# DeltaNet building phase: gate projections beside the substitution, raw blocks in a tile of their own, the second group gathered ahead

## The reference, cut to what matters

```
m = where(strict, (k*beta) @ k.T * decay, 0)
sol = triangular_solve(m + I, [v*beta, k*beta*exp(cum)], lower, unit_diagonal)
attn = where(incl, q @ k.T * decay, 0)
# then step by step over the chunks, with the carried state s:
v_new = u - w @ s;  o = q_dec @ s + attn @ v_new;  s = s*chunk_decay + k_end.T @ v_new
```

## Time and profile before

| | us |
|---|---|
| runs before: median of 3 (lowest, highest) | 2170.61 (2168.0, 2174.12) |
| the profiled execution's own time | 2176.57 |
| its span | 2174.5 |
| mean granted TensorE clock | 0.896 |
| PE busy | 1782.7 (82%) |
| DVE busy | 1175.5 (54%) |
| ACT busy | 837.2 (39%) |
| POOL busy | 321.5 (15%) |

### The profile page before, as it was taken

The page is one execution under the profiler, slowest core; times in us unless marked ns, Lnnn a source line. Parts: engine busy times, 40 slices in busy tenths (PEclk is TensorE's granted clock), DMA queues, the critical chain, the costliest instruction groups (busy, mean ns, idle before and its releaser), DMA issues. The chain is left out here.

```text
span 2174.5 us, 20430 instructions
## 1 busy us (share of the span) xinstructions
PE 1782.7 (82%) x7774; PEld 1221.8 (56%) x7774; DVE 1175.5 (54%) x1356; ACT 837.2 (39%) x1101; POOL 321.5 (15%) x402
## 2 busy tenths in 40 slices
PE   6897889965896838497989889991399999999981
PEld 3344654465454727493434773550288888888861
DVE  3612922168224265364432341337798888888873
ACT  4112222321224426263200000342277777777762
POOL 0000300021000324710040430320011010101000
PEclk9998989978898959798969899995699999999996
DMA  8712000020000442231041213213399999999964
GB/s 348 249 69 79 1 1 0 0 79 1 0 0 0 148 138 85 71 86 67 0 140 39 78 71 134 72 54 126 131 384 395 387 385 402 381 402 386 400 240 174
DMA packets 102569, 337.20 MB, mean 155 GB/s; under 512 B 32170, under 2 KB 41949, under 8 KB 77769
## 3 DMA queue, kind: packets, MB, share of 16 engines
q1 hardware_dynamic: 96048, 317.16, 38.6%
q0 software_dynamic: 4608, 16.78, 3.1%
q10 hardware_dynamic: 1817, 1.97, 0.3%
HBM read 303.83 MB, written 32.04 MB: 154 GB/s over the span
## 5 line engine op out<-in xcount | busy, mean ns | idle before, releaser
L2702 DVE TENSOR_TENSOR w_lo<-w_raw,w_hi 128x2048 fp32r<-128x2048 f32 x192 | 438.5, 2292 | 65.3 <-ACT w_hi L2648 65.2
L2648 ACT ACTIVATE w_hi<-w_raw 128x2048 fp32r<-128x2048 f32 x192 | 367.8, 1917 | 137.4 <-PE ps L2606 134.1
L482 PE MATMUL ps<-hT,w_mixer 128*128 128x512 f32 (+1 forms) x864 | 344.9, 560 | 4.4 <-PEq L186 2.5
L482 PEld LDWEIGHTS ps<-hT,w_mixer 128*128 128x128 f32 x864 | 165.3, 193 | 173.9 <-issue 169.1
L2604 PE MATMUL ps<-w_hi,xsT_hi 128*128 128x512 f32 x512 | 202.8, 396 | 2.4 <-DVE xsT_lo L2707 2.4
L2606 PE MATMUL ps<-w_hi,xsT_lo 128*128 128x512 f32 x512 | 200.4, 391 | 0.0
L2605 PE MATMUL ps<-w_lo,xsT_hi 128*128 128x512 f32 x512 | 200.2, 391 | 0.0
L2431 PE MATMUL ps<-w_out,yT 128*128 128x512 f32 x256 | 114.3, 602 | 3.4 <-DMA router<-in_moe_router 3.4
L2604 PEld LDWEIGHTS ps<-w_hi,xsT_hi 128*128 128x128 f32 x512 | 96.8, 189 | 22.0 <-DVE xsT_lo L2707 2.8
L2606 PEld LDWEIGHTS ps<-w_hi,xsT_lo 128*128 128x128 f32 x512 | 96.5, 189 | 20.3
L2605 PEld LDWEIGHTS ps<-w_lo,xsT_hi 128*128 128x128 f32 x512 | 96.7, 189 | 19.3
(11 more groups left out here) (443 smaller groups left out, 2880.7 us busy)
## 6 DMA issues: line engine op xcount, KB each, us to landing
w_raw<-in_moe_w_gate SPq DMA_DIRECT2D x64, 1024.0 KB, 7.0
w_raw<-in_moe_w_up SPq DMA_DIRECT2D x64, 1024.0 KB, 8.8
w_raw<-in_moe_w_down SPq DMA_DIRECT2D x64, 1024.0 KB, 8.7
w_mod_row<-in_w_mod SPq DMA_DIRECT2D x32, 512.0 KB, 5.0
w_mod<-in_w_mod SPq DMA_DIRECT2D x8, 1024.0 KB, 14.5
dn_ma<-dn_ma SPq DMA_DIRECT2D x16, 512.0 KB, 3.3
dn_rel<-dn_cum SPq DMA_DIRECT2D x20, 256.0 KB, 4.4
dn_mT<-dn_ma SPq DMA_DIRECT2D x20, 256.0 KB, 3.6
```

Source lines behind the costliest of these rows:

```text
L482: last = nc.tensor.matmul(S.ps[:, 3 * (i % 2) + c, 0:n], S.w[:, k, b["col"]:b["col"] + P], S.hT[:, k, t0:t0 + n], start=(k == 0), stop=(k ...
L2648: nc.scalar.activation(wh[q % RING][:, :], S.raw[q % RAW][:, :], ACT.Copy).then_inc(s.hi, 1)
L2702: nc.vector.tensor_tensor(wl[q % RING][:, :], S.raw[q % RAW][:, :], wh[q % RING][:, :].bitcast(F32), ALU.subtract).then_inc(s.lo, 1)
```

## The change

In dn_a, the gate projection of tile 0 is issued by PE ahead of the first unit, and those of tiles 1 to 7 in a row in the pass of unit 12, between the transposes of unit 13 and the k-q product of unit 12. ACT copies the first one out in the pass of unit 0 and the other seven in that of unit 13. POOL's clearing of `B1` goes from the pass of unit 9 to that of unit 13. All gathered blocks land in `bu`, for both directions; `take_blocks` then copies the backward half straight and the forward half transposed into `bl`. After that copy (a new signal, `taken`) `bu` is free, and SP gathers more: units 8 to 10 before it waits for the substitution, then 11 to 13 between the `load_blocks` of the tail. `load_mt` of steps 0 and 1 goes ahead of the wait for the substitution, behind a wait for `zeroed`. In dn_s, SP first gathers only units 14 and 15, and group 2 as soon as POOL has taken group 1, before `load_blocks` of step 3, instead of between the wait for `put_blocks` of group 1 and `load_blocks` of step 4.

```diff
     def gather(sp, n):
-        dst = (bu, bl)[d]
...
-            sp.dma_start(dst[q:q + 4, :, :], ap).then_inc(g_in, 16)
+            sp.dma_start(bu[q:q + 4, :, :], ap).then_inc(g_in, 16)
...
-    def turn_upper(ops):
+    def take_blocks(ops):
+        ops.tensor_copy(bl[64:P, :, :], bu[64:P, :, :])
         return ops.tensor_copy(bl[0:64, :, :], bu[0:64, :, :].rearrange("q r c -> q c r"))
... dn_a, SP
+            sp.wait_ge(s.taken, 1)
+            for n in range(DN_GROUP, HEAD):
+                collect(n)
+            sp.wait_ge(s.zeroed, 1)
+            for st in range(2):
+                load_mt(sp, st)
             sp.wait_ge(s.sub, 1)
             put_blocks(sp, 0, s.d_st)
             for n in range(HEAD, N):
...
-                if m == 1:
-                    sp.wait_ge(s.zeroed, 1)
-                if 1 <= m <= 4:
-                    load_blocks(sp, (m - 1) // 2, (m - 1) % 2)
-                elif m in (5, 6):
-                    load_mt(sp, m - 5)
+                if m in (0, 1, 4, 5):
+                    load_blocks(sp, m // 4, m % 4)
+                elif m in (2, 3, 6):
+                    collect(HEAD + (m - 2 if m < 4 else 2))
... dn_a, PE
+            def gate(t):
+                if t >= 1:
+                    pe.wait_ge(s.og_out, t)
+                for k in range(KD):
+                    last = nc.tensor.matmul(S.ps[:, 7, 0:DG], ...)
+                last.then_inc(s.og, 1)
             pe.wait_ge(S.w_ready, S.w_count)
+            gate(0)
             turn(0)
...
                 if n + 1 < N:
                     turn(n + 1)
+                if n == HEAD + 1:
+                    for g in range(1, LT):
+                        gate(g)
...
-                if n < LT:
-                    (the gate projection of tile n)
... dn_a, ACT
-                if 1 <= n <= LT:
-                    act.wait_ge(s.og, n)
-                    nc.scalar.activation(og[:, n - 1, :], S.ps[:, 7, 0:DG], ACT.Copy).then_inc(s.og_out, 1)
+                for g in range(LT):
+                    if n == (0 if g == 0 else HEAD + 2):
+                        act.wait_ge(s.og, g + 1)
+                        nc.scalar.activation(og[:, g, :], S.ps[:, 7, 0:DG], ACT.Copy).then_inc(s.og_out, 1)
... dn_a, POOL: the memsets of B1
-                if n == LT + 1:
+                if n == HEAD + 2:
... dn_a, DVE
-            ch(turn_upper(nc.vector))
+            take_blocks(nc.vector).then_inc(s.taken, 1)
+            dve.wait_ge(s.taken, 1)
... dn_s, SP
-            for n in range(DN_GROUP, 2 * DN_GROUP):
+            for n in range(HEAD + 3, 2 * DN_GROUP):
                 gather(sp, n)
-                (load_blocks, load_mt and load_attn of step 2 after unit 11)
-            for st in range(3, T):
+            for st in range(2, T):
+                if st == 3:
+                    sp.wait_ge(s.taken, 1)
+                    for n in range(2 * DN_GROUP, N):
+                        gather(sp, n)
                 if st in (4, 8):
...
                     sp.wait_ge(s.d_st, 16 * g)
-                    if g == 1:
-                        for n in range(2 * DN_GROUP, N):
-                            gather(sp, n)
... dn_s, POOL
-                pc(turn_upper(nc.gpsimd))
+                take_blocks(nc.gpsimd).then_inc(s.taken, 1)
+                pool.wait_ge(s.taken, g)
```

More of the change, by code:

```diff
@@ L1346, in deltanet @@
     plan = Plan(nc, mark)
-    with Stage(nc, "dn_a", "r_in*5 e0 e kb kbt kbc kbc_a em kk qk mt at og og_out zeroed cleared sub d_st chain pchain") as s:
+    with Stage(nc, "dn_a", "r_in*5 e0 e kb kbt kbc kbc_a em kk qk mt at og og_out zeroed cleared taken sub d_st chain pchain") as s:
         R = [plan.take(f"dn_rel{i}", [P, HEADS, P]) for i in range(5)]
@@ L1412, in turn @@
                 last.then_inc(s.kbt, 1)
+            def gate(t):
+                if t >= 1:
+                    pe.wait_ge(s.og_out, t)
+                for k in range(KD):
+                    last = nc.tensor.matmul(S.ps[:, 7, 0:DG], S.hT[:, k, (CT + t) * P:(CT + t + 1) * P],
+                                            S.w[:, k, 768:768 + DG], start=(k == 0), stop=(k == KD - 1))
+                last.then_inc(s.og, 1)
             pe.wait_ge(S.w_ready, S.w_count)
+            gate(0)
             turn(0)
@@ L1537, in deltanet @@
     plan = Plan(nc, mark)
-    with Stage(nc, "dn_s", "p5 p_sb pd tb dt rhs y yc z zc dz x tr wt ws vn qo ke kv s_new av o_out zero sub d_st chain "
+    with Stage(nc, "dn_s", "p5 p_sb pd tb dt rhs y yc z zc dz x tr wt ws vn qo ke kv s_new av o_out zero taken sub d_st chain "
                            "pchain") as s:
```

## The result

The changed kernel takes 2145.36 us (median of 4 runs, 2142.77 to 2150.61) against 2170.43 us before in the same series: 25.1 us less, ratio 0.9889 with a 95% interval of 0.9866 to 0.9913. It was forecast at 2137.5 with a range of 2128 to 2150: inside the range, with a quarter of the forecast gain missing.

What follows compares the result with a forecast made beforehand. Bounds: in dn_a the substitution of group 0 on DVE with PE idle, in dn_s POOL's late start on group 1. Sum -10 + 1.5 - 18.2 - 6.4 = -33.1 us, from 2170.6 to 2137.5 us, range 2128 to 2150.

Steps and rivals of the forecast that it cites:

- Step 1: dn_a, units 0 to 10 without gates: 3.5 us a unit from unit 4 on, blocks in 15 us earlier.
- Step 2: dn_a, seven gates beside the substitution of group 0: gates take 31.3 us, `put_blocks` goes out 10 us earlier.
- The pin that the prediction named: dn_a, SP's queue: `put_blocks` held behind the gates by the `zeroed` wait, going out at 782 us.
- Step 3: Tail of dn_a: `load_mt` leaves, twelve gathers enter, costing +1.5 us; tail 24.4 instead of 22.9 us.
- Steps 4 and 5: dn_s: POOL starts group 1 earlier, -18.2 us; group 2's gathers leave the path, -6.4 us.
- The queue rival: dn_a, units 4 to 10: queue and DMAs keep 5.3 us a unit; sum -16, 2154 us; chance 0.12.
- the better case: dn_a: pace 2.98 us, copies at their low ends, no cost in the tail; 2131 us; chance 0.15.
- The slow-gates rival: dn_a: gates run at 1.2 GHz, all 2161 us, half of them 2149 us; chance 0.07.
- the one in which group 1 is not earlier: dn_s: POOL slows beside DVE or the landing is late; sum -15, 2156 us; chance 0.03.
- The slower rival: dn_a: gates pin `put_blocks`, cancelling the gain at 9.2 us a gate; 2177 us at 10 us; chance 0.03.

Runs made afterwards that it cites:

- e5: Changed kernel with two of the four gathers of each of units 0 to 7 issued by ACT, one unit later: 2144.4 us, ratio 0.9863.
- e9: Changed kernel with each of the seven late gate projections computed twice: 2168.8 us, ratio 0.9984.
- e2: Changed kernel with the moves of the gate projections and of POOL's clearing taken back, gathers still ahead: 2150.3 us, ratio 0.9890.
- e3: Changed kernel with `put_blocks` issued ahead of the wait for `zeroed` and the four `load_mt` on SP's queue: 2139.7 us, ratio 0.9855.
- e7: Changed kernel with e3's order and the gathers of units 11 to 13 issued by ACT in its passes of units 17 to 19: 2136.4 us, ratio 0.9828.
- e6: Changed kernel with the gathers of units 11 to 13 issued by ACT in its passes of units 14 to 16: 2146.9 us, ratio 0.9879.

## Why the prediction was right, and where it was off

**Step 1, units 0 to 10 without gates: right way, pace too fast.** Stores of units 4 and 10 are 24.3 us apart, 4.06 us for a unit, where 3.5 was taken between bounds of 2.98 and 4.29. The choice leaned on the DMA work of a unit (3.3 us), but the pace was set by SP and its full queue: e5, with two of the four gathers on another engine's queue, came to 3.05. In a queue that is never empty an issue of a store took 0.7 to 1.6 us, and of the two rows at hand the dearer one (4.29) was the steady state. The blocks were in at 45.8 us after the first decay load instead of 41.8. Of these 4 us `put_blocks` felt only 1.5, since it stands behind the gates and POOL's clearing.

**Step 2, gates beside the substitution: mechanism right.** The gates took 29.8 us, or 30.3 with the last copy (forecast 31.3 with it), at a granted clock of 0.78 in the first and 1.00 in the others; the first took 4.66 us, not 5.96. They ended 2 us ahead of the substitution and not 1 us behind it, since that started later. The forecast counted the last copy twice, once in its 31.3 and once as 0.4. The pin that the prediction named was there: `zeroed` at 774.83 and four `load_mt` ahead of `put_blocks`, 2.2 us behind the substitution. The rule of the Trainium skill (TensorE: Matmul & The Clock Gate, "A second HAM failure mode: psum-queue depth-cycling") did not come true: in this trace, with waits of 0.47 us between groups through one PSUM bank, the clock stayed at its upper level, in e9 too (1.00 from 750 to 796 us). The straight copy on DVE took 0.69 us, as estimated from its table (VectorE: DVE Perf Modes, "The perf-mode tier table (the rule you actually need)"); the trace agrees.

**Step 3, the tail: the term that was mis-sized.** Put at +1.5 us, bounds 0 and 2.5; it measured +6.2, far outside them. The prediction counted SP's issues only. Two things were in its place. First, the exchange of `load_mt` for twelve gathers cost 2.9 us (e2), not 1.5: the issues of the gathers alone took 6.1 us in the changed kernel and not 5.3. Second, 1 MB of `load_mt` was issued right ahead of `put_blocks`, whose landing SP waits for: 6.6 us instead of 2.7. The prediction had counted 1.8 us for issuing them and nothing for the transfers. That wait is the other 3.3 us. e3 took back 4.0 us by swapping the order, 2.6 of them ahead of the tail. This term holds 4.7 of the 5.9 us between the forecast stage sum (-33.1) and the measured one (-27.2). By the medians 8 us of the forecast are missing; the 2 us more are within their interval, which allows a gain of 19 to 29 us.

The time lay inside the range, but not because this term was bounded well: the range had been drawn up to 2150 for other cases, the full queue and slow gates, and that left the room. Its lower end is also added up wrongly: 3 + 1.5 + 2 us below 2137.5 is 2131, not 2129.

**Steps 4 and 5: right.** POOL took group 1 with its transposed copy at 10.0 us after the last store's issue (forecast 10.5), after a straight copy of 1.03 us (taken 1.5); the substitution itself kept its length, 37.1 us, beside steps 0 to 3 of the scan. The gathers of group 2 cost nothing where they are: 6.4 us left the path, and nothing waited for step 3. The idle time ahead of step 4 was 7.1 us, forecast 6.8.

**The rivals.** The queue rival (pace stays at 5.3 us) did not come, though its reason, the backed-up queue, was partly right: 4.06. Of the better case neither the pace of 2.98 nor the free tail came. The slow-gates rival did not come, nor did the one in which group 1 is not earlier: POOL's 37.1 us stood. The slower rival gave a break-even at 9.2 us for a gate; e9, at 7.65 us, came to 277.3 of 279.2 us. Its slope (one us of `put_blocks` for one us of gates) is shown; carried on from e9, the break-even is estimated at 7.65 + 1.9/7 = 7.9 us.

## What to carry to other kernels

Work moved into the shadow of a long stage pays only up to what is queued behind its end: look at what the first small transfer after the stage has ahead of it, and put the one that somebody waits for first. When a limit is taken away, price the next pace by the rows where the queue was full, not by the work in the transfers: issues got longer in a full queue here, and a second engine's queue could carry part of them as long as the waits did not stand ahead of that engine's own chain (e5 and e7 against e6). A move of DMAs is not priced by its issues alone: here they gave +1.5 us and the move cost +6.2, so count also the bytes that the next awaited transfer stands behind.

## What the runs showed of the hardware

- SP's issue of a 512 KB store took 0.34 us on an idle queue and 0.7 to 1.6 us in units 4 to 10 of the changed kernel, where the queue was never empty. Two issuing engines, SP and ACT in e5, moved the same blocks at 3.05 instead of 4.06 us for a unit, with the share of the DMA engines up from 0.73 to 0.88.
- A 512 KB transfer issued behind 1 MB on the same queue landed after 6.6 us (changed kernel); with nothing ahead of it, after 2.7 us (kernel before, e2) and 2.9 us (e3).
- PE at 3.72 us of work and 0.47 us of waiting kept a granted clock of 1.00 for 25 us (46 us in e9, with 7.17 us of work), while in units 4 to 10 of the changed kernel, where it was busy 19.5 of 24.4 us in short groups of products, it was granted 0.51.
- The part of the program ahead of the change took between 701.5 and 709.2 us in executions of programs that are identical there.
